# Time mixing's keys and the up projections in seven quarter products, with weight sums on GpSimd

## The chip, the cores and the metric

The kernel runs on one core of one Trainium2 chip. The metric is the device time of one execution in microseconds. The kernel's matmul, vector, activation and GpSimd engines are called TensorE (PE), VectorE (DVE), ScalarE (ACT) and GpSimd (POOL) below; SyncE (SP) issues the loads of the weights.

## The reference

All is fp32. A sequence of 256 tokens with 1024 features passes through two blocks. The first has window attention, spatial gating, pooling, memory attention and a feed-forward. The second puts 16 meta tokens in front (272 tokens) and has two layers, RWKV-7 time mixing and stick-breaking attention, each followed by a feed-forward with a short convolution. What the change touches is this:

```
# time mixing: keys
xk = x + (token_shift(x) - x) * mix[2]
k = xk @ w_k                                   # 272 x 1024 by 1024 x 1024
kk = heads(k * k_k); kk = kk / max(norm(kk), 1e-12)

# feed-forward, once per layer
u = rms_norm(h) @ w_up                         # by 1024 x 5632
u = conv_width_3(u, per channel) + conv_b
gate, val = split(u)
h = h + (silu(gate) * val) @ w_down            # 2816 x 1024
```

## The kernel before

Features lie on the 128 partitions and tokens along the free axis. All weights are one stream of blocks of 128 x 1024 (512 KB), which SyncE loads in order into a ring of eight; block b is loaded as soon as block b-8 is used. A block holds the weights of one output tile of 128 features: 8 k tiles of 128 x 128. The order of all work is written out by hand, engine by engine, with semaphores: `second_tensor`, `second_vector` and `second_scalar` hold the queues of the second block.

**Full products.** `tiles` (and the inner loop of `ffn`) does one output tile as 8 matmuls of 272 columns (260 in the last layer, where 12 meta tokens are no longer needed). The results wait in a PSUM bank for VectorE.

**Seven products.** A pair of output tiles, seen as a 2 x 2 matrix of quarters (k in two interleaved halves, output tiles in two), times x in quarters (k halves, token halves) is done as seven quarter products (Strassen-Winograd) instead of eight. `Seven` holds the layout: first block, tokens of a half, PSUM banks for even and odd pairs, first pair `i0`, and `step`. `weight_sums` makes four sums of weight quarters for each pair (lines 865, 867, 868, 870, 128 x 512 each) into one of two buffers; `x_sums` makes four sums of x once; `seven_products` issues 7 x 4 matmuls of half the columns (136 or 130) and waits for the sums before the products 6, 7 and 3; ScalarE copies the first product (`keep_first_product`, line 852), and VectorE puts the quarters together (`quads_scaled`, lines 1574 to 1580: five additions that read PSUM and one product with the norm's root). TensorE may begin pair i when pair i-2 has been taken (`taken`). Before the change the keys of time mixing are eight full tiles, and in the up projections, with F2 = 22 pairs (a gate tile and a value tile each), every odd pair is done in seven (`step` 2) and every even one in full.

**Feed-forward, up stage.** For pair m VectorE takes the result from PSUM times the norm's root (line 1643, or `quads_scaled`), for odd m makes the weight sums of pair m+2, then waits for ScalarE's first tap with bias (line 1312), adds two taps for each of the two tiles (line 1651, four instructions), waits for ScalarE's silu (line 1315) and multiplies (line 1659). After m = 3, 7, 11, 15, 19 and 21 it makes the x sums of the down projection (lines 875 to 878). In the last two pairs it makes the first two of the down projection's weight sums. The down projection (`seven_products(.., down)`) has 11 k tiles a half, in groups of 4, 4 and 3; each group waits for its x sums and its weight sums.

**Time mixing around the keys.** TensorE: r tiles 4 to 7 with the small products (`lora_out`) between, the eight key tiles, the first value tile, a sum over heads of the squared keys (16 small matmuls, `kk_sum`), more value tiles, and the chunked scan. VectorE copies r, scales and scans the decays (line 1439), takes the keys (line 1444), scales them (line 1446). ScalarE does three exponentials (line 1253 and next) after the scans and squares the keys (line 1257).

GpSimd has 32 instructions in the whole kernel, all in the first block and before time mixing.

Of the kernel before, what the change touches and what calls it, by code (L numbers as in the profile page):

```python
# [32 lines left out]
GB = 4  # L33
# [187 lines left out]
def program(nc, stream, x_t, mem_t, meta_t, cols_d, consts_d, sinks_d, ws_t, b_sp, w_pool,  # L221
            w1_d, a1_d, g1_d, w2_d, a2_d, g2_d, out_t):
    with ExitStack() as ctx:
# [142 lines left out]
        for name, y, sums in (("gate", Seven(FIRST["in"] + 18, P, [4], (0, 2), TIGHT, 0, GATES, 0, True), 1),  # L366
                              ("upq", Seven(FIRST["up"], P, [4], (3, 0), WIDE_UP, UH // 2, FF // 2, -UH, True), 1),
                              ("down", Seven(FIRST["down"], P, [4] * 4, (4, 0), SPLIT, 0, 4, 0, True), 4),
                              ("rw_o", Seven(FIRST["rw_o"], T2, [4], (0, 4), SPLIT, 1, 4, GB, True), 1),
                              ("ffa_up", Seven(FIRST["ffa_up"], T2, [4], (0, 4), WIDE, 1, F2, GB, True, 2), 1),  # L370
                              ("ffa_down", Seven(FIRST["ffa_down"], T2, [4, 4, 3], (4, 0), SPLIT, 0, 4, 0, True), 6),
                              ("sb_k", Seven(FIRST["sb_k"], T2, [4], (4, 0), WIDE, 1, 4, GB, True), 1),
                              ("sb_q", Seven(FIRST["sb_v"], L2 // 2, [4], (4, 0), WIDE, 0, 4, GB, False), 2),
                              ("sb_o", Seven(FIRST["sb_o"], L2 // 2, [4], (0, 4), SPLIT, 1, 4, GB, True), 1),
                              ("ffb_up", Seven(FIRST["ffb_up"], L2 // 2, [4], (0, 4), WIDE, 1, F2, GB, True, 2), 1),
                              ("ffb_down", Seven(FIRST["ffb_down"], L2 // 2, [4, 4, 3], (4, 0), SPLIT, 0, 4, 0, True), 6)):
            y.pair0, y.group0, y.sums0 = n_pairs, n_groups, n_sums
            SEVEN[name] = y
            n_pairs, n_groups = n_pairs + len(y.pairs()), n_groups + len(y.groups) * len(y.pairs())
            n_sums += sums  # L380

# [114 lines left out]

        def x_quarters(name):
# [31 lines left out]
        act2m = Marks(sem("time_mix_act"), "tw heads_kept tg tg1 kk_squared tg1_moved kk_root")  # L529
# [81 lines left out]
        def second_tensor(pe, mm, tiles, total):  # L611
# [73 lines left out]
            for n in range(KT):  # L685
                tiles("rw_k", FIRST["rw_k"] + n, 1, xm[1], L, j0=n)
            pe.wait_ge(ev["rw_k"], GB + 8)
            pe.wait_ge(mixed, 3)

            def value_block(n, at, freed):  # L690
                tiles("rw_v", FIRST["rw_v"] + n, 1, xm[2], L, j0=n)
                if n == 0:
                    act2m.wait(pe, "tg1_moved")
                lora_out(16 + n, beside(at), freed, g2s, tg0[:, :], g2t, tg1[0:32, :])
# [66 lines left out]
            def ffn(name, i, before):  # L761
# [3 lines left out]
                for m in range(F2):  # L765
                    if m % 2:
                        if m == 3:
                            pe.wait_ge(rooted, 10 + i)
                        seven_products(pe, mm, up, only=m)
                        continue  # L770
                    for s in (2 * m, 2 * m + 1):
                        b = FIRST[up] + s
                        arrived(pe, b)
                        if s == 1:
                            pe.wait_ge(ev[before], GB + 8)
                        elif m:
                            pe.wait_ge(ev[up], GB + s - 3)
# [34 lines left out]
        def seven_products(pe, mm, name, second=None, only=None, within=None):  # L812
# [5 lines left out]
            for i in y.pairs() if only is None else (only,):  # L818
# [4 lines left out]
                for g, n in enumerate(y.groups):  # L823
# [11 lines left out]
                    for p in ORDER:  # L835
                        if p in (6, 7, 3):
                            pe.wait_ge(w_summed, done + {6: 2, 7: 3, 3: 4}[p])
# [16 lines left out]
        def weight_sums(dve, tt, name, i, g):  # L854
# [15 lines left out]
            tt(s4, a12, s2, ALU.subtract).then_inc(w_summed, 1)  # L870

# [344 lines left out]
        def second_scalar(act, link, f, root):  # L1216
# [33 lines left out]
            for n in range(KT):  # L1250
                if n == 2:
# [4 lines left out]
                act.wait_ge(ev["rw_k"], GB + n + 1)  # L1256
                last = f(xx[:, n, :], k2[:, n, :], ACT.Square, scale=col("k_k", n))
                if n == KT - 1:
                    act2m.reach(last, "kk_squared")
            act.wait_ge(used, FIRST["rw_k"] + 8)  # L1260
            act2m.reach(cp(tg1[0:32, :], tg1_first[0:32, :]), "tg1_moved")
            value_kept(0)
# [36 lines left out]
        def ffn_scalar(act, f, root, name, layer, which):  # L1299
# [5 lines left out]

            for m in range(F2):
                if m % 2:
                    keep_first_product(act, name + "_up", m)
# [5 lines left out]
                act.wait_ge(conv_done, layer * 2 * F2 + 2 * m + 1)  # L1314
                f(cu[:, (2 * m) % 4, :], cu[:, (2 * m) % 4, :], ACT.Silu).then_inc(ffs, 1)  # L1315
# [84 lines left out]
        def second_vector(dve, link, v, tt, stt, ts, inverse_root, take):  # L1400
# [34 lines left out]
            take_r(4, KT)  # L1435
# [4 lines left out]
            link(ins)  # L1440
            tt(epre, cum, lw, ALU.subtract).then_inc(decays_summed, 1)
            for n in range(KT):
                dve.wait_ge(used, FIRST["rw_k"] + n + 1)
                cpv(k2[:, n, :], gps(n % GB)).then_inc(ev["rw_k"], 1)
                dve.wait_ge(ev["rw_k"], GB + n + 1)
                ts(kkn[:, n, :], k2[:, n, :], col("k_k", n), None, ALU.mult)
# [180 lines left out]
        def ffn_vector(dve, link, tt, stt, name, layer, quads_scaled):  # L1627
# [7 lines left out]
            for m in range(F2):  # L1635
                if m % 2:
                    quads_scaled(up, m, uu[:, (2 * m) % 4:(2 * m) % 4 + 2, :])
                    if m + 2 < F2:
                        weight_sums(dve, tt, up, m + 2, 0)
                else:  # L1640
                    for s in (2 * m, 2 * m + 1):
                        dve.wait_ge(used, b + s + 1)
                        tt(uu[:, s % 4, :], gps(3 + 4 * (s % 2), width), rs[:, 0:width], ALU.mult).then_inc(ev[up], 1)
                if m >= F2 - 2:
                    weight_sums(dve, tt, down, 0, m - F2 + 2)
                for s in (2 * m, 2 * m + 1):
                    dve.wait_ge(ffc, layer * 2 * F2 + s + 1)
                    for back, tap in ((1, 1), (2, 0)):
# [4 lines left out]
                        if back == 1:  # L1653
                            link(ins)
                        else:
                            ins.then_inc(conv_done, 1)
                dve.wait_ge(conv_done, layer * 2 * F2 + 2 * m + 2)
                dve.wait_ge(ffs, layer * F2 + m + 1)
                tt(act2[:, m, :], cu[:, (2 * m) % 4, :], cu[:, (2 * m + 1) % 4, :], ALU.mult).then_inc(ffm, 1)
                if m % 4 == 3 or m == F2 - 1:  # L1660
                    dve.wait_ge(ffm, layer * (2 + F2) + 2 + m + 1)
                    x_sums(link, tt, down, slice(m // 4 * 2, (m + 1) // 2))

# [983 lines left out]
        def _(pool):  # L2647
# [38 lines left out]
            for n in range(2):  # L2686
# [7 lines left out]
                else:  # L2694
                    pool2.reach(ins, "wa_scaled")

# [83 lines left out]
```

## Time and profile before

| | us |
|---|---|
| median of 3 runs (1451.17 to 1454.74) | 1454.0 |
| the profiled execution, own time | 1446.48 |
| its span | 1444.7 |
| TensorE busy | 1410.2 (98%) |
| TensorE weight loads (beside the products) | 1288.4 (89%) |
| VectorE busy | 911.2 (63%) |
| ScalarE busy | 326.7 (23%) |
| GpSimd busy | 26.6 (2%) |
| mean granted TensorE clock, share of full | 0.994 |
| DMA | 190.73 MB, mean 132 GB/s |

Busy times are of the span, from one profiled execution. Stages by TensorE's timeline: time mixing from 528 to 775, keys from 570.1 to 600.2, first feed-forward's up stage from 816.9 to 969.9, second one's from 1217.7 to 1365. An engine's idle time costs nothing unless another engine waits for what it does.

### The profile page before, as it was taken

To read this page: it belongs to the slowest core of one execution; us is meant where nothing else is said; L and a number is where in the kernel's file an instruction comes from. 1 tells how busy PE (TensorE), PEld (TensorE's weight loads), DVE (VectorE), ACT (ScalarE), POOL (GpSimd) and SP (SyncE) were. 2 spreads that over 40 slices of the span, in tenths; PEclk is the share of its full clock that TensorE was granted. 3 is DMA by queue.
4 is the path that set the end of the run, shared out by engine and by line. 5 is a ranking of instruction groups with operands and counts; after the bars stand their busy time and mean duration, and the time that the engine had idled before them with its cause. 6 is when DMAs were issued, how large, how long until landed. Compare 5 with 4: busy or idle time off the path is not lost.

```text
span 1444.7 us, 30444 instructions
## 1 busy us (share of the span) xinstructions
PE 1410.2 (98%) x12960; PEld 1288.4 (89%) x12960; DVE 911.2 (63%) x1836; ACT 326.7 (23%) x656; POOL 26.6 (2%) x32
## 2 busy tenths in 40 slices
PE   9999999999999999998899999999999999999997
PEld 8899888999999977778787989999997779999997
DVE  3288433358865473568544887887684447878875
ACT  2134103250000131420121222220103642222211
POOL 0140000000001000000000000000000000000000
PEclk9999999999999999999999999999998999999999
DMA  9435344355444413320000444445543114445451
GB/s 371 161 133 166 113 161 145 117 165 193 166 163 169 158 50 128 131 88 4 5 4 2 147 160 137 169 147 175 187 137 116 52 36 137 158 145 174 149 192 69
DMA packets 56992, 190.73 MB, mean 132 GB/s; under 512 B 9216, under 2 KB 11392, under 8 KB 56608
## 3 DMA queue, kind: packets, MB, share of 16 engines
q1 hardware_dynamic: 50768, 180.93, 37.1%
q10 hardware_dynamic: 6096, 7.91, 1.7%
q8 instruction: 102, 1.67, 0.5%
q14 instruction: 26, 0.21, 0.0%
HBM read 187.77 MB, written 1.05 MB: 131 GB/s over the span
## 4 chain that ended last, share of the span: by engine, by line
PE 93%; DVE 3%; ACT 1%; issue 1%; DMA 0%; ACTq 0%; DVEq 0%; PEldq 0%
PE ps L1886 93%; DVE arena L1674 1%; DMA arena<-in_x_t 0%; DVE arena L1701 0%; PE ps L1171 0%; DVE rs L2371 0%; ACT arena L2319 0%; DVE arena L1702 0%; DVE arena L1625 0%; PE ps L2089 0%; PE ps L1980 0%; DVE arena L1580 0%; DVE arena L865 0%; DVE arena L867 0%; DVE arena L1685 0%
## 5 line engine op out<-in xcount | busy, mean ns | idle before, releaser
L1886 PE MATMUL ps<-arena,ring 128*128 128x128 f32 (+6 forms) x4752 | 819.6, 324 | 3.0 <-PEq L806 0.8
L1886 PEld LDWEIGHTS ps<-arena,ring 128*128 128x128 f32 x4752 | 718.2, 191 | 75.5 <-issue 7.8
L1886 PE MATMUL ps<-arena 64*64 64x64 f32 (+10 forms) x6982 | 572.4, 257 | 13.9 <-issue 6.6
L1886 PEld LDWEIGHTS ps<-arena 128*128 128x128 f32 (+4 forms) x6982 | 514.7, 162 | 44.7 <-issue 23.9
L865 DVE TENSOR_TENSOR arena<-ring 128x512 f32<-128x512 f32 x100 | 69.0, 690 | 119.6 <-PE ps L1886 86.8
L852 ACT COPY arena<-ps 128x128 f32<-128x128 f32 (+2 forms) x72 | 19.2, 266 | 336.9 <-PE ps L1886 336.9
L1651 DVE SCALAR_TENSOR_TENSOR arena<-arena,cols 128x271 f32<-128x271 f32 (+3 forms) x176 | 82.8, 492 | 9.8 <-ACT arena L1312 6.7
L1886 PE MATMUL ps<-arena,consts 128*128 128x260 f32 (+9 forms) x368 | 75.1, 346 | 7.3 <-DVE arena L1829 3.0
L1312 ACT ACTIVATE arena<-arena,cols 128x272 f32<-128x272 f32 (+1 forms) x88 | 48.8, 601 | 122.8 <-DVE arena L1580 68.9
L1886 PEld LDWEIGHTS ps<-arena,consts 128*128 128x128 f32 (+3 forms) x368 | 54.3, 182 | 21.9 <-issue 3.5
L867 DVE TENSOR_TENSOR arena<-arena,ring 128x512 f32<-128x512 f32 x100 | 69.6, 696 | 3.5
L870 DVE TENSOR_TENSOR arena<-ring,arena 128x512 f32<-128x512 f32 x100 | 69.4, 694 | 0.0
L868 DVE TENSOR_TENSOR arena<-ring 128x512 f32<-128x512 f32 x100 | 68.6, 686 | 0.0
L2371 DVE RECIPROCAL rs<-rs 128x256 f32<-128x256 f32 (+2 forms) x10 | 17.9, 1786 | 32.7 <-ACT rs L2187 32.7
L1296 ACT ACTIVATE arena<-res 128x272 f32<-128x272 f32 (+1 forms) x32 | 13.6, 424 | 107.9 <-DVE res L1548 79.7
L1574 DVE TENSOR_TENSOR arena<-arena,ps 128x130 f32<-128x130 f32 (+1 forms) x29 | 8.5, 292 | 43.3 <-PE ps L1886 43.3
L1315 ACT ACTIVATE arena<-arena 128x272 f32<-128x272 f32 (+1 forms) x44 | 18.7, 425 | 67.9 <-DVE arena L1651 67.9
L1821 DVE TENSOR_TENSOR arena<-arena,ps 128x840 f32<-128x840 f32 x8 | 8.2, 1029 | 30.0 <-PE ps L1886 30.0
L1695 DVE TENSOR_TENSOR arena<-ps,consts 128x512 f32<-128x512 f32 x23 | 15.7, 688 | 12.3 <-PE ps L1886 12.1
L2277 ACT ACTIVATE arena<-arena 128x256 f32<-128x256 f32 (+1 forms) x12 | 5.8, 486 | 74.4 <-DVE arena L2514 66.0
L1580 DVE TENSOR_TENSOR arena<-arena,rs 128x520 f32<-128x520 f32 (+1 forms) x29 | 20.7, 712 | 3.0
L1701 DVE TENSOR_TENSOR arena<-arena,ps 128x512 f32<-128x512 f32 x18 | 12.3, 685 | 13.4 <-PE ps L1886 13.4
(279 smaller groups left out, 894.8 us busy)
## 6 DMA issues: line engine op xcount, KB each, us to landing
ring<-in_stream SPq DMA_DIRECT2D x342, 512.0 KB, 3.8
consts<-in_consts ACTq DMA_DIRECT2D x1, 1580.0 KB, 12.9
arena<-in_mem_t ACTq DMA_DIRECT2D x1, 1024.0 KB, 7.3
res<-in_x_t ACTq DMA_DIRECT2D x1, 1024.0 KB, 19.2
out_t<-arena SPq DMA_DIRECT2D x4, 256.0 KB, 2.5
arena<-in_x_t ACTq DMA_DIRECT2D x3, 256.0 KB, 5.0
arena<-in_g ACTq DMA_DIRECT2D x1, 640.0 KB, 5.6
arena<-in_w ACTq DMA_DIRECT2D x2, 256.0 KB, 4.5
```

What stands on the lines that cost most here:

```text
L852: nc.scalar.copy(QUADS[name][y.turn(i)][:, 0, 0:y.t], product_at(y, i, 1)).then_inc(p1_kept, 1)
L865: tt(s1, a21, a22, ALU.add).then_inc(w_summed, 1)
L867: tt(s2, s1, a11, ALU.subtract).then_inc(w_summed, 1)
L868: tt(s3, a11, a21, ALU.subtract).then_inc(w_summed, 1)
L870: tt(s4, a12, s2, ALU.subtract).then_inc(w_summed, 1)
L1312: f(cu[:, s % 4, :], uu[:, s % 4, :], ACT.Identity, scale=cols[:, wc + s:wc + s + 1], bias=cols[:, bc + s:bc + s + 1]).then_inc(ffc, 1)
L1315: f(cu[:, (2 * m) % 4, :], cu[:, (2 * m) % 4, :], ACT.Silu).then_inc(ffs, 1)
L1580: tt(dst, dst, over(rs[:, at], 2), ALU.mult).then_inc(ev[name], 2)
L1651: ins = stt(out=c, in0=uu[:, s % 4, 0:width - back], scalar=cols[:, at:at + 1], in1=c, op0=ALU.mult, op1=ALU.add)
L1695: tt(ysb[c % 2], blocks(2 * (c % 2) + 1), over(const(f"level{m}"), KT), ALU.mult).then_inc(y_masked[c % 2], 1)
L1886: return nc.tensor.matmul(out, lhs, rhs, start=start, stop=stop)
L2371: link(v.reciprocal(rs[:, 0:t], rs[:, 0:t]))
```

## The change

The keys become four pairs in seven products, with their own places for sums in space that is free then. In both up projections `step` becomes 1, so all pairs but the first (m = 0) are in seven products: 10 more pairs in each. The weight sums of pairs 2 to 21 move to GpSimd (`up_weight_sums`), which counts on a semaphore of its own; VectorE's counter is moved past them by hand (`count_gpsimd_sums`). VectorE's order in the up stage becomes: take pair m, gate product of m-2, taps of m-1; ScalarE's: copy of the first product of m, first taps of m, silu of m-1. In time mixing VectorE gets x sums, weight sums and `quads_keys`; ScalarE's squares go behind all keys, and its exponentials ahead of the copy of the last pair.

```diff
+    ("rw_k", Seven(FIRST["rw_k"], T2, [4], (0, 4), WIDE, 0, 4, GB, True), 1),
-    ("ffa_up", Seven(FIRST["ffa_up"], T2, [4], (0, 4), WIDE, 1, F2, GB, True, 2), 1),
+    ("ffa_up", Seven(FIRST["ffa_up"], T2, [4], (4, 0), WIDE, 1, F2, GB, True), 1),
-    ("ffb_up", Seven(FIRST["ffb_up"], L2 // 2, [4], (0, 4), WIDE, 1, F2, GB, True, 2), 1),
+    ("ffb_up", Seven(FIRST["ffb_up"], L2 // 2, [4], (4, 0), WIDE, 1, F2, GB, True), 1),
...
# TensorE, keys
-            for n in range(KT):
-                tiles("rw_k", FIRST["rw_k"] + n, 1, xm[1], L, j0=n)
-            pe.wait_ge(ev["rw_k"], GB + 8)
+            seven_products(pe, mm, "rw_k", lambda: pe.wait_ge(ev["lora"], GB + 16))
+            pe.wait_ge(ev["rw_k"], GB + 6)
...
# GpSimd
+        def up_weight_sums(pool, tt, name):
+            y = SEVEN[name]
+            for i in range(2, F2):
+                b, done = y.block(i), sums_before(name, i)
+                a11, a12, a21, a22 = w_quarters(b)
+                s1, s2, s3, s4 = [WSUM[name][y.group(i, 0) % 2][:, x] for x in range(4)]
+                arrived(pool, b)
+                arrived(pool, b + 1)
+                pool.wait_ge(used, y.block(i - 1 if i >= 3 else 0))
+                tt(s1, a21, a22, ALU.add).then_inc(ups_summed, 1)
+                pool.wait_ge(ups_summed, done + 1)
+                tt(s2, s1, a11, ALU.subtract).then_inc(ups_summed, 1)
+                tt(s3, a11, a21, ALU.subtract).then_inc(ups_summed, 1)
+                pool.wait_ge(ups_summed, done + 2)
+                tt(s4, a12, s2, ALU.subtract).then_inc(ups_summed, 1)
...
# ScalarE, up stage
             for m in range(F2):
-                if m % 2:
+                if m:
                     keep_first_product(act, name + "_up", m)
...
-                act.wait_ge(conv_done, layer * 2 * F2 + 2 * m + 1)
-                f(cu[:, (2 * m) % 4, :], cu[:, (2 * m) % 4, :], ACT.Silu).then_inc(ffs, 1)
+                if m:
+                    silu(m - 1)
+            silu(F2 - 1)
...
# VectorE, keys
+            dve.wait_ge(mixed, 3)
+            x_sums(link, tt, "rw_k")
+            take_r(4, 5)
+            weight_sums(dve, tt, "rw_k", 0, 0)
+            take_r(5, 6)
+            weight_sums(dve, tt, "rw_k", 1, 0)
+            take_r(6, KT)
...
+            weight_sums(dve, tt, "rw_k", 2, 0)
+            quads_keys(0)
+            quads_keys(1)
+            weight_sums(dve, tt, "rw_k", 3, 0)
             tt(epre, cum, lw, ALU.subtract).then_inc(decays_summed, 1)
+            quads_keys(2)
+            scaled_keys(0, 6)
...
+            quads_keys(3)
+            scaled_keys(6, 8)
# VectorE, up stage
+            for m in range(F2):
+                if m:
+                    quads_scaled(up, m, uu[:, (2 * m) % 4:(2 * m) % 4 + 2, :])
+                else:
+                    for s in range(2):
+                        dve.wait_ge(used, b + s + 1)
+                        tt(uu[:, s, :], gps(3 + 4 * s, width), rs[:, 0:width], ALU.mult).then_inc(ev[up], 1)
+                if m >= 2:
+                    gate(m - 2)
+                if m >= 1:
+                    convolve(m - 1)
+                if m >= F2 - 2:
+                    weight_sums(dve, tt, down, 0, m - F2 + 2)
+            gate(F2 - 2)
+            convolve(F2 - 1)
+            gate(F2 - 1)
```

## Rows read from the trace of the kernel before

**Rows 1.** The page: busy time by engine, and the chain that ended last.
```profile
PE 1410.2 (98%) x12960; PEld 1288.4 (89%) x12960; DVE 911.2 (63%) x1836; ACT 326.7 (23%) x656; POOL 26.6 (2%) x32
...
PE 93%; DVE 3%; ACT 1%; issue 1%; DMA 0%; ACTq 0%; DVEq 0%; PEldq 0%
```
**Rows 2.** Timeline, TensorE, first up stage: start, us, engine, line, operation, count.
```profile
831.65 8.42 PE L1886 MATMUL ps<-arena,ring 128*128 128x272 f32 x40
839.91 2.02 PE L1886 MATMUL ps<-arena 128*128 128x136 f32 x16
...
845.47 8.42 PE L1886 MATMUL ps<-arena,ring 128*128 128x272 f32 x40
```
**Rows 3.** Timeline, TensorE, second up stage.
```profile
1232.12 8.07 PE L1886 MATMUL ps<-arena,ring 128*128 128x260 f32 x40
1240.03 1.95 PE L1886 MATMUL ps<-arena 128*128 128x130 f32 x16
...
1245.39 8.07 PE L1886 MATMUL ps<-arena,ring 128*128 128x260 f32 x40
```
**Rows 4.** Timeline, VectorE, first up stage.
```profile
824.66 1.85 DVE L2371 RECIPROCAL rs<-rs 128x272 f32<-128x272 f32 x1
...
831.85 0.30 DVE L1574 TENSOR_TENSOR arena<-arena,ps 128x136 f32<-128x136 f32 x1 [1.31 <-PE ps L1886]
...
833.61 0.72 DVE L1580 TENSOR_TENSOR arena<-arena,rs 128x544 f32<-128x544 f32 x1
834.25 0.68 DVE L865 TENSOR_TENSOR arena<-ring 128x512 f32<-128x512 f32 x1
...
836.78 1.97 DVE L1651 SCALAR_TENSOR_TENSOR arena<-arena,cols 128x271 f32<-128x271 f32 x4
838.79 0.44 DVE L1659 TENSOR_TENSOR arena<-arena 128x272 f32<-128x272 f32 x1
...
936.01 0.44 DVE L875 TENSOR_TENSOR arena<-arena 128x272 f32<-128x272 f32 x1
...
937.67 0.78 DVE L1643 TENSOR_TENSOR arena<-ps,rs 128x272 f32<-128x272 f32 x2
```
**Rows 5.** Timeline, all engines but TensorE, where GpSimd works; last, groups by form.
```profile
86.15 0.73 POOL L2671 TENSOR_TENSOR arena<-arena 128x256 f32<-128x256 f32 x1
86.21 0.42 DVE L2417 TENSOR_TENSOR arena<-arena,ps 128x256 f32<-128x256 f32 x1
...
439.21 0.69 DVE L868 TENSOR_TENSOR arena<-ring 128x512 f32<-128x512 f32 x1
439.44 1.37 POOL L2690 TENSOR_TENSOR arena<-arena,small 128x512 f32<-128x512 f32 x1
439.83 1.52 DVE L870 TENSOR_TENSOR arena<-ring,arena 128x512 f32<-128x512 f32 x1
440.88 1.37 POOL L2691 TENSOR_TENSOR arena<-arena,small 128x512 f32<-128x512 f32 x1
442.33 1.04 POOL L2690 TENSOR_TENSOR arena<-arena,small 128x512 f32<-128x512 f32 x1
...
L2653 POOL TENSOR_TENSOR arena<-arena 128x512 f32<-128x512 f32 x1 | 1.3, 1267 | 0.1
```
**Rows 6.** Timeline, TensorE, VectorE and ScalarE around the keys.
```profile
570.06 29.60 PE L1886 MATMUL ps<-arena,ring 128*128 128x272 f32 x128
600.20 3.93 PE L1886 MATMUL ps<-arena,ring 128*128 128x272 f32 x16 [0.53 <-DVE arena L1444]
...
605.17 1.12 PE L1886 MATMUL ps<-arena,consts 128*32 128x272 f32 x16
...
577.37 2.42 DVE L1441 TENSOR_TENSOR arena<-arena 128x2176 f32<-128x2176 f32 x1
...
581.46 1.28 ACT L1253 ACT_TABLE_LOAD   x1
582.75 2.02 ACT L1253 ACTIVATE arena<-arena 128x2176 f32<-128x2176 f32 x1
```

More of the change, by code:

```diff
@@ L380, in program, with sums_by_gpsimd, sums_before @@
             n_sums += sums
+        ups_summed = sem("up_weights_summed")
+        def sums_by_gpsimd(name, i):
+            return name in ("ffa_up", "ffb_up") and i >= 2
+        def sums_before(name, i):
+            return 4 * ((F2 - 2) * (name == "ffb_up") + i - 2)
         def product_at(y, i, p, more=1):
@@ L1249, in second_scalar @@
                 lora_kept(j, 4 + j % GB)
-            for n in range(KT):
-                if n == 2:
+            for i in range(4):
+                if i == 3:
                     act.wait_ge(decays_summed, 1)
@@ L1255, in second_scalar @@
                     f(epre, epre, ACT.Exp).then_inc(decays_up, 1)
[L1256 to L1259, printed above, removed]
+                keep_first_product(act, "rw_k", i)
             act.wait_ge(used, FIRST["rw_k"] + 8)
             act2m.reach(cp(tg1[0:32, :], tg1_first[0:32, :]), "tg1_moved")
+            for n in range(KT):
+                act.wait_ge(ev["rw_k"], GB + 2 * (n // 2) + 2)
+                last = f(xx[:, n, :], k2[:, n, :], ACT.Square, scale=col("k_k", n))
+            act2m.reach(last, "kk_squared")
             value_kept(0)
@@ L1434, in second_vector, with quads_keys, scaled_keys @@
             mix(3, 2)
-            take_r(4, KT)
+            dve.wait_ge(mixed, 3)
[5 more added lines that the diff above has]
+            take_r(6, KT)
+            def quads_keys(i):
+                y = SEVEN["rw_k"]
+                q = QUADS["rw_k"][y.turn(i)]
+                p1, u2, uv = q[:, 0, :], q[:, 1, :], q[:, 2:4, :]
+                quarters = k2[:, 2 * i:2 * i + 2, :].rearrange("p a (b t) -> p (a b) t", b=2)
+                two = lambda p: product_at(y, i, p, 2).rearrange("p (a t) -> p a t", a=2)
+                dve.wait_ge(used, y.block(i + 1))
+                dve.wait_ge(p1_kept, y.pair(i) + 1)
+                link(tt(u2, p1, product_at(y, i, 6), ALU.add))
+                tt(quarters[:, 2, :], p1, product_at(y, i, 2), ALU.add)
+                link(tt(uv, two(7), over(u2, 2), ALU.add))
+                tt(quarters[:, 0:4:3, :], uv, two(4), ALU.add)
+                tt(quarters[:, 1, :], uv[:, 0, :], product_at(y, i, 5), ALU.add).then_inc(ev["rw_k"], 2)
+            def scaled_keys(n0, n1):
+                dve.wait_ge(ev["rw_k"], GB + n1)
+                for n in range(n0, n1):
+                    ts(kkn[:, n, :], k2[:, n, :], col("k_k", n), None, ALU.mult)
             dve.wait_ge(ev["lora"], GB + 15)
@@ L1440, in second_vector @@
             link(ins)
+            weight_sums(dve, tt, "rw_k", 2, 0)
+            quads_keys(0)
+            quads_keys(1)
+            weight_sums(dve, tt, "rw_k", 3, 0)
             tt(epre, cum, lw, ALU.subtract).then_inc(decays_summed, 1)
[L1442 to L1446, printed above, removed]
+            quads_keys(2)
+            scaled_keys(0, 6)
+            dve.wait_ge(ev["lora"], GB + 16)
             link(tt(same_head, ident, const("centre"), ALU.subtract))
             ts(same_head, same_head, 64.0, None, ALU.mult)
+            quads_keys(3)
+            scaled_keys(6, 8)
             dve.wait_ge(ev["lora"], GB + 16)
@@ L1634, in ffn_vector, with convolve @@
             up, down = name + "_up", name + "_down"
[L1635 to L1645, printed above, removed]
+            count_gpsimd_sums(dve, up)
+            def convolve(m):
                 for s in (2 * m, 2 * m + 1):
@@ L1656, in ffn_vector, with gate @@
                             ins.then_inc(conv_done, 1)
+            def gate(m):
                 dve.wait_ge(conv_done, layer * 2 * F2 + 2 * m + 2)
```

30 lines of the change are left out of this document (24 added, 6 removed).

## The prediction

> **What bounds the kernel now.** I read the page's busy line and chain of waits first. TensorE is busy for 98% of the span and carries 93% of the chain that ends last; VectorE has 3% [rows 1]. So a change pays what it takes off TensorE's own stream, as long as nothing else becomes late. The second view is the timeline of TensorE, for the price of a pair of output tiles in both forms. One fp32 matmul stands there as two instructions, so a full pair (2 tiles, 8 k, 272 columns) is 32 and a pair in seven products (7 products, 4 k, 136 columns) is 56. From 831.65 to 845.47 a full pair and a pair of seven follow one another without a gap: 13.82 us. In it the six products after the first take from 839.91 to 845.47, 5.56 us or 0.927 each, so seven take 6.49 and the full pair 7.33 [rows 2]. In the second feed-forward (260 columns) the same pattern takes 13.27, with six products in 5.36: 6.25 for seven, 7.02 for the full pair [rows 3]. The third view is VectorE's timeline of one pair, since each pair of seven gives VectorE work [rows 4].
>
> **Part 1, the keys.** Eight key tiles go from 570.06 to 599.66 (29.60 us, of which the 128 instructions need 29.3) and then TensorE waits until 600.20 for the last tile to be copied [rows 6]. Four pairs of seven at 6.49 end at 596.0; the next matmul waits only for pair 2, long taken. That is 4.2 us earlier. New VectorE work there is four quarter sums and 16 weight sums at 0.6 each; I queue them by the code: two sets lie in VectorE's idle time beside the r tiles, set 2 goes at 577.34, where the scans end (L1441 starts at 577.37 [rows 6]), and set 3 at 585.0, done 587.5, before pair 3 starts at 589.5. None is late. What moves is ScalarE: its three exponentials wait for decays_summed, now at 589.9 instead of 579.8. They took 2.0 each behind a table load of 1.28 [rows 6], 7.2 in all with their overlap, so they end at 597.1, and the copy of pair 3's first product, queued behind them, makes VectorE's last quads end at 599.2 and the squares of the keys at 601.3. TensorE wants these for the kk sum, which stood at 605.17 [rows 6], at 600.6: 0.7 lost. The kk sum then runs at 601.4, so I take **-3.8 us** (ends: -4.2 with no wait; -1 if the reciprocal on VectorE that follows the kk sum is late too). Value and scan stages keep their order behind it.
>
> **Part 2, the products of the up projections.** Ten more pairs in each. 10 x (7.33 - 6.49) = 8.4 and 10 x (7.02 - 6.25) = 7.7: **-16.1 us** [rows 2, 3]. Parts 1 and 2 together: -19.9, if all is hidden.
>
> **Part 3, VectorE beside them.** Per pair it now needs: the quarter sums and the scaling, 831.85 to 834.25, 2.40; the four taps, 836.78 to 838.79, 2.01; the gate product at 838.79, 0.4; and every fourth pair the sums for the down projection, 936.01 to 937.67, 1.66, a quarter of it 0.42 [rows 4]. That is 5.2 of the 6.49 us that a pair now lasts (5.0 of 6.25 in the second). So with the weight sums (834.25 to 836.78, 2.53 [rows 4]) gone to GpSimd, VectorE has 1.3 us a pair to spare; with them it would have had 7.7, too much.
>
> **Part 4, GpSimd and what it does to VectorE.** This decides the sign. 20 pairs in each stage, 4 additions of 512 each: 160 instructions. Undisturbed, GpSimd takes 1.04 us for such a one (two inputs, 512), and 1.27 in another place [rows 5]. Four with 0.08 between them are 4.5 to 5.4 us, under 6.49, and TensorE needs a set only a pair later: GpSimd alone is no bound.
> But the two engines are not independent. At 439.83 VectorE's L870, always 0.69 otherwise, takes 1.52 and ends at 441.35. GpSimd's addition of 512 ran from 439.44 to 440.81, itself 1.37 instead of 1.04: it began to read when L868 had read its last element, about 439.8. Of such an instruction some 0.53 us go by its elements (0.68 for 512, 0.44 for 272 [rows 4]), so L870 read from about 440.7. GpSimd's next, at 440.88, again took 1.37: it sat behind L870 [rows 5]. The two take turns, a whole instruction at a time, and GpSimd holds the way for about 0.9 us of its 1.04. At 86.15 a GpSimd addition ran beside VectorE's L2417, whose one operand is in PSUM, and neither was longer (0.73, 0.42) [rows 5]: it holds for VectorE instructions with both inputs in SBUF.
> The Trainium skill (SBUF — State Buffer, Who interferes with whom) says the same: a VectorE instruction with two SBUF inputs contends with a GpSimd instruction that reads SBUF, and whoever has the shared port pair keeps it for the whole instruction. This speaks against the change more than GpSimd's own speed does, and by that rule the trace agrees. GPSIMD Engine Reference, Engine selection, puts elementwise work on VectorE because GpSimd is about 2x slower with two inputs; here 1.04 against 0.69 is 1.5x, and by its 2x (1.38 an instruction, an estimate from that page) a set would take 5.8, still under a pair.
> Which of VectorE's 5.2 us can be stopped? The five quarter sums read PSUM (1.76 us, 831.85 to 833.61 [rows 4]); the scaling by rs, the taps, the gate and the down sums read only SBUF: 3.4 us, two thirds. A GpSimd instruction that meets them costs VectorE at most its 0.9, and about 0.75 since start and tail of VectorE's instructions lie beside it. Bounds per pair: 0, and 4 x 0.9 = 3.6. I take two thirds of 4 x 0.75: 2.0. VectorE then needs **7.2 us a pair** against TensorE's 6.49, and 7.0 against 6.25 in the second. TensorE may not start pair i before pair i-2 is scaled (two sets of banks), so VectorE may be 6.49 - 2.45 = 4 us late and then sets the pace; and what it is late at the end, the down projection waits for, since its sums stand in the same queue. So the lag is paid in full: 20 x 0.7 = 14 and 20 x 0.75 = 15, **+29 us**.
>
> **Part 5, start and end of each up stage.** GpSimd's first set starts with the stage (its weights are there), just where VectorE does weight sums and x sums, ready at 824.66 for a pair of seven that starts at 831.65 - 6.49 = 825.16 [rows 2, 4]: 0.5 to spare. Four turns at about 0.5 cost 2.1: +1.6 each. At the end the order gate(m-2), taps(m-1) leaves two tap groups and two gates, and both weight sets of the down projection (2 x 2.53), behind the last pair. By the queue the second set's second sum comes at 9.0 us after the last pair, and TensorE wants it at 6.49 + 0.93 = 7.4: +1.6 each. Bounds 0 and 4 each. Together **+6.4 us**. The new order on ScalarE (activation one pair later) I cost at nothing: it is busy for 23% of the span [rows 1].
>
> **Sum.** -3.8 - 16.1 + 29 + 6.4 = **+16 us** on the profiled execution (span 1444.7, its own time 1446.5), thus 1462 there. Taken on the median shown, 1454.0, which is 7.5 above that execution: **about 1471 us**, 1.1% slower.
>
> **Rivals.**
> A, the forecast: VectorE, stopped by GpSimd, paces both up stages. For: the turns that the two engines took, three of them in one place [rows 5]. Against: the 2.0 us of blocking is worked out, not seen, and the sign turns at about 1.35 us a pair. Its own range is 1460 to 1488. Chance 0.58.
> B, other side: the stops fall mostly beside the PSUM reads and in the 1.3 us to spare, since each GpSimd set starts when a pair ends, as the quarter sums do. If VectorE's lag stays under 4 us, only start and end cost: -19.9 + 3 to 6, about **1438 to 1441**. It decides if blocking is under 1.3 us a pair (1.25 in the second). For: the first two of four additions do start beside the quarter sums. Against: the other two then meet scaling, gate and taps, and every fourth pair has no room at all (4.8 + 1.66 = 6.4). Chance 0.27.
> C, in between: one stage paced by VectorE and not the other, or blocking near 1.4: 1448 to 1459. Chance 0.07.
> D, GpSimd at 1.27 an addition as in its slowest case: 1.1 held, 2.6 blocked a pair, 0.6 x 40 = 24 more: about **1495**. GpSimd itself would use 5.4 plus its own stops, close to the 6.49. Chance 0.08.
>
> **Numbers.** Predicted is A: 1471. The range runs from B to A's end: 1437 to 1490; it leaves out D and little else. A measurement here tells 0.3% (4.4 us) from no change. Faster is B, 0.27. Same is half of C and little more, 0.07. Slower 0.66.
>
> **What would show it.** For A: waits of TensorE in both up stages for the scaling at L1580, in pieces of 1 to 4 us and mostly behind the pairs with down sums; the taps' mean up from 0.49 to 0.7 or more, GpSimd's additions at 1.1 to 1.3. For B: no such waits, taps under 0.65. Part 1 is right if the first value tile starts some 26 us after the first key product and ScalarE's last copy of a first key product comes right after the exponentials. Part 5 is right if TensorE waits once at the first pair of seven and once in the second group of the down projection. The prediction is wrong at its root if VectorE's SBUF-only instructions in the up stages keep their durations.

## The result, and the profile after

The changed kernel took **1509.9 us** (median of 4 runs, 1507.5 to 1512.1) against 1452.6 for the kernel before (4 runs, 1445.3 to 1454.7): a ratio of 1.041, 95% interval 1.038 to 1.044. It is slower by 57 us; 1471 was predicted, with 1490 as the upper end. The direction was right, the size was not, and the time lies outside the range.

The page of the changed kernel: the busy line, and the chain that ended last by engine and by line.

```profile
PE 1418.1 (94%) x13536; PEld 1318.9 (87%) x13536; DVE 1020.5 (68%) x1868; ACT 326.8 (22%) x680; POOL 249.9 (17%) x192
...
PE 73%; DVE 20%; issue 5%; ACT 1%; DMA 0%; DVEq 0%; ACTq 0%; SPq 0%; PEldq 0%
```

TensorE's share of the chain fell from 93% to 73% and VectorE's rose from 3% to 20% [rows 1]. VectorE's busy time rose by 109 us. Its own work fell by 80 weight sums in the up stages and rose by 16 for the keys and 24 sets of quarter sums; the added and the spared work nearly cancel, and the rise is instructions that last longer.

Where the time went is read from TensorE's timeline: the first product of the sums over features at the start of each stage marks it. Of the changed kernel, start and duration:

```profile
816.47 1.08 PE L1972 MATMUL ps<-arena,consts 128*128 128x272 f32 x4
...
1070.35 1.08 PE L1972 MATMUL ps<-arena,consts 128*128 128x272 f32 x4
```

That is the first feed-forward, 253.9 us; the marks of the second stand at 1249.80 and 1499.02, 249.2 apart. The same marks of the kernel before stand 224.3 and 213.6 apart. So the two feed-forwards lost 29.6 and 35.7 us, 65 together, and all else together gained 1.

What TensorE waited for most (the changed kernel; us in total, times, longest), and some of the waits themselves in the first feed-forward (x8 is eight instructions, which are four matmuls):

```profile
PE ps L1972 <- DVE arena L1656: 47.9, 12, 6.2
```

```profile
823.56 1.17 PE L1972 MATMUL ps<-arena,ring 128*128 128x136 f32 x8 [2.35 <-DVE arena L919]
...
877.91 2.18 PE L1972 MATMUL ps<-arena,ring 128*128 128x136 f32 x8 [5.02 <-DVE arena L1656]
...
977.86 2.18 PE L1972 MATMUL ps<-arena,ring 128*128 128x136 f32 x8 [5.04 <-DVE arena L1656]
...
1002.42 2.12 PE L1972 MATMUL ps<-arena 128*128 128x136 f32 x16 [1.21 <-DVE arena L888]
```

L1656 is the scaling by the root (L1580 before), L919 the last x sum, L888 the second of the four weight sums of a set of the down projection. The list has no wait of TensorE for a GpSimd sum: GpSimd's sums are never late. After two smaller ones at 858.51 and 866.14 the waits come every fourth pair (877.91, 910.66, 944.08, 977.86), 5 us each, and between 877.91 and 977.86 twelve pairs pass: 8.33 us a pair, where TensorE needs 6.49 and the forecast had 7.2. In the second feed-forward the same waits stand at 1309.52 and 1411.58: 8.51 a pair, where 7.0 was forecast.

VectorE in 850 to 990, grouped by form (count | busy us, mean ns):

```profile
L1719 DVE SCALAR_TENSOR_TENSOR arena<-arena,cols 128x271 f32<-128x271 f32 x34 | 29.1, 856 | 0.0
L1719 DVE SCALAR_TENSOR_TENSOR arena<-arena,cols 128x270 f32<-128x270 f32 x34 | 25.9, 761 | 1.2
L1656 DVE TENSOR_TENSOR arena<-arena,rs 128x544 f32<-128x544 f32 x17 | 19.0, 1116 | 1.8
L1729 DVE TENSOR_TENSOR arena<-arena 128x272 f32<-128x272 f32 x17 | 17.0, 999 | 0.0
L1653 DVE TENSOR_TENSOR arena<-arena,ps 128x272 f32<-128x272 f32 x17 | 7.5, 439 | 0.6
...
L917 DVE TENSOR_TENSOR arena<-arena 128x272 f32<-128x272 f32 x4 | 5.6, 1395 | 0.1
```

The quarter sums, which read PSUM, kept their duration (L1653: 439 ns, the same as a 272-column instruction had before). All that takes both its inputs from SBUF is longer: the taps 0.81 instead of 0.50, the scaling 1.12 instead of 0.72, the gate product 1.00 instead of 0.44 [rows 4]. Per pair that is 1.24 for four taps, 0.39 for the scaling and 0.56 for the gate; the four down sums of every fourth pair (L916 to L919) took 4.7 instead of 1.66, 0.71 a pair (12 us over 17 pairs). Together **2.9 us a pair**, against the 2.0 of the forecast. The second feed-forward gives 3.1 by the same sum (1281 to 1415, 16 pairs).

The other engine, GpSimd's weight sums over the whole kernel (lines 906, 908, 909 and 911, 40 sets; L909 has 1475 and L906 1369 ns), and a piece of both engines' timelines, GpSimd first:

```profile
L911 POOL TENSOR_TENSOR arena<-ring,arena 128x512 f32<-128x512 f32 x40 | 59.0, 1475 | 0.0
...
L908 POOL TENSOR_TENSOR arena<-arena,ring 128x512 f32<-128x512 f32 x40 | 53.6, 1340 | 3.1
```

```profile
886.34 1.27 POOL L906 TENSOR_TENSOR arena<-ring 128x512 f32<-128x512 f32 x1 [7.37 <-PE ps L1972]
887.69 1.27 POOL L908 TENSOR_TENSOR arena<-arena,ring 128x512 f32<-128x512 f32 x1
888.92 1.75 POOL L909 TENSOR_TENSOR arena<-ring 128x512 f32<-128x512 f32 x1
```

```profile
882.84 0.73 DVE L1656 TENSOR_TENSOR arena<-arena,rs 128x544 f32<-128x544 f32 x1
883.48 0.43 DVE L1729 TENSOR_TENSOR arena<-arena 128x272 f32<-128x272 f32 x1
883.84 1.98 DVE L1719 SCALAR_TENSOR_TENSOR arena<-arena,cols 128x271 f32<-128x271 f32 x4
...
887.97 1.58 DVE L1656 TENSOR_TENSOR arena<-arena,rs 128x544 f32<-128x544 f32 x1
889.47 1.50 DVE L1729 TENSOR_TENSOR arena<-arena 128x272 f32<-128x272 f32 x1
```

Until 886.34 GpSimd is idle and VectorE's instructions last as before. From then on it works; its first addition meets the quarter sums, which read PSUM, and the same two instructions behind them last 1.58 and 1.50. Undisturbed, an addition takes GpSimd **1.27 us, not 1.04**. Both figures stood in [rows 5].

### The profile page after: what moved, and what is told of

Same layout as the page of the kernel before. It is cut to its first block, busy times and chain, and to the rows that moved or that the text cites. A ratio compares the mean times of both kernels' runs of the same rounds, so it can differ in the third digit from the quotient of the medians.

```text
span 1508.8 us, 31889 instructions
## 1 busy us (share of the span) xinstructions
PE 1418.1 (94%) x13536; PEld 1318.9 (87%) x13536; DVE 1020.5 (68%) x1868; ACT 326.8 (22%) x680; POOL 249.9 (17%) x192
## 4 chain that ended last, share of the span: by engine, by line
PE 73%; DVE 20%; issue 5%; ACT 1%; DMA 0%; DVEq 0%; ACTq 0%; SPq 0%; PEldq 0%
PE ps L1972 72%; DVE arena L1719 5%; DVE arena L1729 2%; DVE arena L1656 1%; DVE arena L1653 1%; DVE arena L918 1%; DVE arena L917 1%; DVE arena L919 1%; DVE arena L1652 1%; DVE arena L916 1%; DVE arena L1651 1%; DVE arena L1650 1%; DVE arena L1760 1%; DVE arena L886 1%; DVE arena L888 1%
## 5 line engine op out<-in xcount | busy, mean ns | idle before, releaser
L1972 PE MATMUL ps<-arena,ring 128*128 128x128 f32 (+6 forms) x4560 | 735.7, 311 | 55.8 <-DVE arena L1656 47.9
L1972 PEld LDWEIGHTS ps<-arena,ring 128*128 128x128 f32 x4560 | 652.1, 194 | 104.9 <-DVE arena L1656 50.8
L1972 PE MATMUL ps<-arena 64*64 64x64 f32 (+8 forms) x7750 | 684.8, 262 | 17.4 <-issue 7.5
L1972 PEld LDWEIGHTS ps<-arena 128*128 128x128 f32 (+4 forms) x7750 | 620.8, 168 | 48.9 <-issue 25.0
L906 POOL TENSOR_TENSOR arena<-ring 128x512 f32<-128x512 f32 x40 | 54.7, 1369 | 738.2 <-PE ps L1972 738.2
L1719 DVE SCALAR_TENSOR_TENSOR arena<-arena,cols 128x271 f32<-128x271 f32 (+3 forms) x176 | 135.5, 790 | 3.1
L888 DVE TENSOR_TENSOR arena<-arena,ring 128x512 f32<-128x512 f32 x84 | 59.5, 708 | 2.9
L911 POOL TENSOR_TENSOR arena<-ring,arena 128x512 f32<-128x512 f32 x40 | 59.0, 1475 | 0.0
L909 POOL TENSOR_TENSOR arena<-ring 128x512 f32<-128x512 f32 x40 | 59.0, 1475 | 0.0
L1656 DVE TENSOR_TENSOR arena<-arena,rs 128x520 f32<-128x520 f32 (+1 forms) x49 | 51.4, 1050 | 5.5 <-DVE arena L1654 0.5
L908 POOL TENSOR_TENSOR arena<-arena,ring 128x512 f32<-128x512 f32 x40 | 53.6, 1340 | 3.1
L1729 DVE TENSOR_TENSOR arena<-arena 128x272 f32<-128x272 f32 (+1 forms) x44 | 38.0, 864 | 0.1
```

The source lines that it names most:

```text
L888: tt(s2, s1, a11, ALU.subtract).then_inc(w_summed, 1)
L906: tt(s1, a21, a22, ALU.add).then_inc(ups_summed, 1)
L908: tt(s2, s1, a11, ALU.subtract).then_inc(ups_summed, 1)
L909: tt(s3, a11, a21, ALU.subtract).then_inc(ups_summed, 1)
L911: tt(s4, a12, s2, ALU.subtract).then_inc(ups_summed, 1)
L1656: tt(dst, dst, over(rs[:, at], 2), ALU.mult).then_inc(ev[name], 2)
```

## The experiments

Each run is compared with the kernel before on the same chip. "Expected" is what was put on record before the run, "stages" the changes of the first and the second feed-forward against before, by the marks above, from each run's profile. Executions of one kernel spread by up to 16 us (e6, 12 runs: 1437.9 to 1454.3).

| run | expected us | median us | ratio to before (95%) | stages |
|---|---|---|---|---|
| the changed kernel | about 1471 | 1509.9 | 1.041 (1.038 to 1.044) | +29.6, +35.7 |
| e1 keys only | 1448.5 | 1444.3 | 0.996 (0.994 to 0.998) | 0, 0 |
| e2 sums over 32 of 512 | 1433 to 1441 | 1429.4 | 0.986 (0.981 to 0.992) | -6.8, -5.6 |
| e3 writes, no reads | 1433 to 1442 | 1435.9 | 0.989 (0.984 to 0.993) | -6.8, -5.6 |
| e5 root in PSUM | 1496 to 1506 | 1489.5 | 1.026 (1.022 to 1.031) | +24.4, +18.1 |
| e8 one operand twice | 1470 to 1485 | 1478.7 | 1.018 (1.012 to 1.024) | +13.8, +16.0 |
| e4 all sums on VectorE | 1484 to 1492 | 1479.4 | 1.019 (1.016 to 1.022) | +13.3, +16.5 |
| e6 17 pairs in seven | 1441 to 1446 | 1440.8 | 0.996 (0.993 to 0.998) | -2.0, +1.1 |
| e7 15 pairs in seven | 1442 to 1445 | 1446.3 | 0.996 (0.994 to 0.998) | -1.0, -0.2 |
| e9 as e6, weight set early | 1435 to 1437, or 1441 | 1444.3 | 0.996 (0.994 to 0.998) | -1.9, 0.0 |
| e10 as e7, weight set early | about 1442, or 1446 | 1449.2 | 0.999 (0.996 to 1.001) | -0.9, +1.5 |

e2, e4 and e5 came out 4 to 7 us below what was expected (e4 and e5 in every execution), and no run shows why; e7 came out 1 us above.

### e1: the keys alone

The feed-forwards are those of the kernel before; only the keys are in seven.

> The kernel before with the keys of time mixing in four pairs of seven products, nothing else of the change. The first value tile started 30.14 us after the first key product before and 26.05 after, so 4.1 us should be won and kept: 1448.5, ratio 0.997. If the value and scan stages behind it take the gain back: ratio 1.000.

Measured: 1444.3 against 1451.2 (12 and 29 runs), -6 us by the ratio (-3 to -9). The term of the forecast, -3.8, lies inside. The mark behind the scan stage varies by 10 us between profiles of kernels that agree up to there (813.3 in e1, 823.6 in e3), so the changed kernel's own timeline is the finer measure:

```profile
571.89 1.20 PE L1972 MATMUL ps<-arena,ring 128*128 128x136 f32 x8
...
597.94 3.83 PE L1972 MATMUL ps<-arena,ring 128*128 128x272 f32 x16
601.61 1.27 PE L1972 MATMUL ps<-arena 128*128 128x272 f32 x4
602.81 1.12 PE L1972 MATMUL ps<-arena,consts 128*32 128x272 f32 x16
```

The first value tile starts 26.05 us after the first key product, against 30.14 [rows 6], and the kk sum follows 30.92 after it against 35.11, with no wait: -4.2.

### e2 and e3: the sums made small, or without reads

```
+                few = [x[:, :, 0:8] for x in (s1, s2, s3, s4, a11, a12, a21, a22)]
+                s1, s2, s3, s4, a11, a12, a21, a22 = few
```

> The changed kernel, but GpSimd's four sums of each pair cover 8 of 128 columns of a quarter (32 elements instead of 512); the rest of the sum buffers holds old values. Same instructions, waits and order on all engines, hardly any reading by GpSimd. Theory T (GpSimd's reads stop VectorE's instructions with both inputs in SBUF, a whole instruction at a time, and VectorE so slowed paces both up stages): almost all of the loss goes, 1433 to 1441 us, taps at L1719 back to 0.50 mean, no waits of TensorE for the scaling at L1656. Rival R (the new order on VectorE and ScalarE, or seven products in all pairs, is too much for VectorE by itself): stays above 1480. Rival G (GpSimd is late with its sums): also about 1437, so it needs the next run.

```
-                tt(s1, a21, a22, ALU.add).then_inc(ups_summed, 1)
+                nc.gpsimd.memset(s1, 0.5).then_inc(ups_summed, 1)
```

(and so for s2, s3, s4)

> The changed kernel with GpSimd's four sums replaced by four fills of the same 512 elements (it writes the buffers and reads nothing); values of the sums are not made. T: writing does not stop VectorE's reads, 1433 to 1442 us although GpSimd still has 160 instructions of full width. If any work of GpSimd slows VectorE, also writing: above 1470, taps above 0.65 us.

In e2 the waits for the scaling are gone and the order of all queues is the changed kernel's. The only waits of the up stages left in it:

```profile
PE ps L1974 <- DVE arena L888: 2.6, 2, 1.4
```

They stand at the ends of the two stages; at their starts none is left. So neither the new order nor the amount of VectorE's own work made the changed kernel slow: with GpSimd's reads away it is 1.4% faster than before, and 80 us faster than with them. In e3 GpSimd works on the same 128 x 512, but only writes. GpSimd's and VectorE's groups (of the whole kernel):

```profile
L911 POOL MEMSET arena<- 128x512 f32 x40 | 21.1, 527 | 0.0
...
L1719 DVE SCALAR_TENSOR_TENSOR arena<-arena,cols 128x271 f32<-128x271 f32 x44 | 21.8, 495 | 0.0
```

The taps last what they lasted before, and so does the scaling (725 ns) [rows 4]. It is the reads that stop VectorE, not these writes (a fill is also shorter, 0.53 us against the addition's 1.27, but 2.1 us of fills a pair lengthen nothing). The Trainium skill (SBUF — State Buffer, Who interferes with whom) says this of a VectorE instruction with two SBUF inputs: it contends with a GpSimd instruction that reads SBUF and not with one that only writes it. By that rule the trace agrees.

### e5: the scaling reads its root from PSUM

```
-                    quads_scaled(up, m, uu[:, (2 * m) % 4:(2 * m) % 4 + 2, :])
+                    quads_scaled(up, m, uu[:, (2 * m) % 4:(2 * m) % 4 + 2, :], gps(3, width))
+                    dve.wait_ge(ev[up], GB + 2)
+                    link(nc.vector.tensor_copy(gps(3, width), rs[:, 0:width]))
```

> The changed kernel; VectorE copies the norm's root once into a PSUM bank that is free after the first pair and takes it from there when it scales each pair, so this instruction (L1656, 544 elements, 1.12 mean in the middle of the first up stage against 0.72 undisturbed) has one SBUF input instead of two. T: it goes back to 0.73 while GpSimd works beside it; part of the stop moves to the gate product and the taps behind it: 0.2 to 0.4 us a pair are won, 1496 to 1506 us. If it is not the inputs in SBUF that matter but VectorE's time in general: L1656 stays above 1.0 and the time within 0.3% of the changed kernel's 1509.

```profile
L1719 DVE SCALAR_TENSOR_TENSOR arena<-arena,cols 128x271 f32<-128x271 f32 x44 | 40.0, 909 | 0.0
...
L1656 DVE TENSOR_TENSOR arena<-arena,ps 128x544 f32<-128x544 f32 x21 | 15.1, 721 | 2.2
```

The scaling, in the two up stages 1.10 on average with both inputs in SBUF, takes 0.72 (0.70 in the second) again, as when nothing disturbs it; the taps behind it are still stopped, and more. The gain is 20 us, more than the 4 to 14 expected. Over both up stages the scaling is 17 us shorter than in the changed kernel, the gate products are 10 and the down sums 4 shorter, and the taps 15 longer: 16 us less on VectorE. The waits for the scaling became 15, the longest 4.2 instead of 6.2; shorter waits also leave TensorE fewer slow matmuls (below), which would explain the rest, but no run separates it.

### e8: GpSimd's additions with one operand read twice

```
-                tt(s1, a21, a22, ALU.add).then_inc(ups_summed, 1)
+                tt(s1, a21, a21, ALU.add).then_inc(ups_summed, 1)
```

(and so for the others)

> The changed kernel; each of GpSimd's four sums takes one of its operands twice (a21+a21 and so on), so the values of the sums differ, the number of elements does not. In the changed kernel an undisturbed sum takes 1.26, while the rows of the forecast had 1.04 for 512 elements where both operands were nearly the same addresses or one was a few broadcast values. If that is what makes 1.04 of 1.26: mean undisturbed duration 1.04, blocking about 2.0 to 2.4 a pair instead of 2.9, and the time falls to 1470 to 1485, near the forecast. If two reads are two reads wherever they go: 1.26 again and 1509 within 0.5%.

Its timeline, GpSimd (first undisturbed, then not) and VectorE beside it:

```profile
853.98 1.04 POOL L908 TENSOR_TENSOR arena<-arena 128x512 f32<-128x512 f32 x1
854.98 1.52 POOL L909 TENSOR_TENSOR arena<-ring 128x512 f32<-128x512 f32 x1
```

```profile
854.66 0.94 DVE L1656 TENSOR_TENSOR arena<-arena,rs 128x544 f32<-128x544 f32 x1
855.53 1.27 DVE L1729 TENSOR_TENSOR arena<-arena 128x272 f32<-128x272 f32 x1
```

This is the forecast's assumption made true: an undisturbed addition of 1.04 us (in three of the four lines; the fourth, L911, was never under 1.22). The gate product behind one lasts 1.27 instead of 0.43, 0.84 more, where the forecast allowed 0.75. By the same sum as above VectorE is stopped for 2.2 us a pair in the first stage (850 to 990) and 2.3 in the second (1275 to 1400). The time, 1478.7, is 7.7 above the 1471 predicted and inside the forecast's own range (1460 to 1488). 31 of the 39 us that the forecast missed hang on what one addition costs, with what follows from longer stops.

### e4: all sums on VectorE

GpSimd has no sums; VectorE makes the set of pair m+2 after it has taken pair m, as in the kernel before, for all pairs but the first.

```
+            def sums_of_nth(n):
+                if n < len(SEVEN[up].pairs()):
+                    weight_sums(dve, tt, up, SEVEN[up].pairs()[n], 0)
...
                     quads_scaled(up, m, uu[:, (2 * m) % 4:(2 * m) % 4 + 2, :])
+                    sums_of_nth(SEVEN[up].nth(m) + 2)
```

> The changed kernel with all weight sums of the up projections on VectorE, two pairs ahead, right after it has taken a pair; GpSimd does none. VectorE then needs 5.2 + 2.5 = 7.7 us a pair for certain, against 5.2 plus a measured 2.9 of stops with GpSimd. T: GpSimd costs VectorE more than it takes off it, so this is faster than the changed kernel: 20 x 1.25 and 20 x 1.3 us of lag on 1432.4 (all hidden), and 3 at the ends: 1484 to 1492. Rival (GpSimd relieves VectorE, the loss lies elsewhere): slower than 1510.

It is faster than the changed kernel by 30 us, although VectorE does all the work, and 5 us faster than was expected. TensorE's waits for the scaling in its first up stage:

```profile
873.44 1.19 PE L1998 MATMUL ps<-arena,ring 128*128 128x136 f32 x8 [0.95 <-DVE arena L1674]
...
965.09 1.19 PE L1998 MATMUL ps<-arena,ring 128*128 128x136 f32 x8 [1.80 <-DVE arena L1674]
```

Two more stand between them, the longest 2.02. Twelve pairs in 91.65 us are 7.64 a pair; the forecast said 7.7 for this case and dismissed it. In the changed kernel GpSimd takes 2.5 us a pair of work from VectorE and gives back 2.9 of stops.

### e6, e7, e9 and e10: fewer pairs in seven

With all sums on VectorE, full pairs are put back where it would be late: `FULL = (0, 5, 9, 13, 17)` in e6, `FULL = (0, 3, 6, 9, 12, 15, 18)` in e7.

> Keys in seven; in each up projection 17 of 22 pairs in seven (full ones: 0, 5, 9, 13, 17) instead of 11, all weight sums on VectorE, GpSimd none, order of the changed kernel. TensorE: 4.1 + 6 x 0.84 + 6 x 0.77 = 13.8 less. VectorE: 17 x 7.7 + 5 x 3.6 = 149 us against TensorE's 147 in a stage: about 2 us late at each end, plus 1 to 2 for the sums of the down projection. T: 1441 to 1446, ratio 0.992 to 0.996. If VectorE at its limit loses more than the sum says (chains between engines): 1450 or more.

> As the one with seventeen, with 15 of 22 pairs in seven (full: 0, 3, 6, 9, 12, 15, 18). TensorE: 4.1 + 4 x 1.61 = 10.5 less. VectorE: 15 x 7.7 + 7 x 3.6 = 141 of 149 us, so it is not late in the stage: 1442 to 1445, ratio 0.993 to 0.995; the three pairs of seven at the end, with both weight sets of the down projection, may cost 1 to 2.

Both have the ratio of e1: the six and four additional pairs of a stage brought next to nothing. Their waits in the middle of the stage are gone, what is left stands at its end. Of e6 (e7 has the same at 970.86, 1.90 us, and in the second stage 2.20):

```profile
968.67 2.12 PE L1998 MATMUL ps<-arena 128*128 128x136 f32 x16 [2.20 <-DVE arena L906]
```

L906 belongs to the down projection's second weight set, behind a gate product, four x sums and four taps in VectorE's queue (4.0 us, 963.18 to 967.20, not the 5.3 of the expectation below). In e9 and e10 it goes ahead of them:

```
+                if m == F2 - 1:
+                    weight_sums(dve, tt, down, 0, 1)
                 if m >= 2:
                     gate(m - 2)
```

> Keys and 17 of 22 pairs in seven as in the run with full pairs 0, 5, 9, 13, 17, all sums by VectorE; only the down projection's second weight set moves ahead of the gate product, the sums of activations and the taps that stood before it in the last pair (5.3 us of VectorE's queue). If the order at the end of the up stage is what took the rest of the gain, TensorE's waits for L906 (5.7 us, 3 times, longest 2.3 in that run) fall under 2 us and the time is 4 to 6 us less than that run's 1440.8: about 1435 to 1437. If VectorE's load itself is the limit there, the wait comes back a pair later, for the sums of activations, and the time stays within 2 us of 1441.

> The same move in the kernel with full pairs 0, 3, 6, 9, 12, 15, 18 (15 of 22 in seven). If the order at the end is the cause, its waits for L906 (4.1 us, 2 times) go and the stages, -1.0 and -0.2 us against before, come to about -3.2 and -2.3: the time some 4 us under that run's 1446.3 or, by the profiles' spans, 1436. By the rival it stays.

```profile
979.72 0.93 PE L2000 MATMUL ps<-arena,ring 128*128 128x136 f32 x6 [2.00 <-DVE arena L937]
980.96 1.66 PE L2000 MATMUL ps<-arena 128*128 128x136 f32 x12 [0.30 <-DVE arena L906]
```

The wait of e9 stands one group later, for the last x sum (L937), and is nearly as long, and its first stage gains as much as that of e6: the rival's mechanism is there, at 1444.3 instead of the 1441 that it gave. e10 has the same waits (1.70 and 2.10 us). What VectorE has left after the last pair is more than TensorE's next work covers, in both orders that were tried. The kernel before, whose VectorE has less to do there, has no such wait in either feed-forward. In e6 the stages fall 3.0 and 5.7 us short of what TensorE's sums gave, 8.7 together. The three waits for L906 are 5.7 of it. Another 1.6 are slow matmuls behind the last of them: at 1363.04 sixteen instructions took 3.51 instead of 1.95. The remaining 1.4 stays unexplained. By the ratios none of the four is told apart from e1, so **the keys alone are the version to keep**: 0.4% faster than before, with nothing added to the up projections.

## Why the prediction was right or wrong

**Part 1, the keys: right.** -3.8 was said, -4.2 measured, since the kk sum did not wait. The expected order on ScalarE is there: the exponentials run from 592.31 to 598.14 and the copy of the last first product stands right behind them, at 598.05.

**Part 2, TensorE's own saving: right.** The pairs go at 6.49 and 6.25 wherever nothing stops them. e2 shows it nearly whole: -12.4 in the two stages against the saving of -16.1. Of the missing 3.7 the waits for L888 at the two ends are 2.6; nothing waits at the starts, and 1.1 stays open.

**Part 3, VectorE's own need: right.** 5.2 a pair; in e2 taps, scaling and gate last what was taken, and no wait for the scaling is left.

**Part 4, the stops: the mechanism right, the size wrong, and this is the step that failed.** Turns of whole instructions, only against VectorE instructions that take both inputs from SBUF, waits of TensorE for the scaling behind the pairs with down sums (5 us, where 1 to 4 were said), taps at 0.7 or more: all there (taps 0.79). The failed term is what one addition costs, "Undisturbed, GpSimd takes 1.04 us for such a one", and with it the 0.75 of a stop and the 2.0 of a pair: the additions take 1.27 undisturbed, and 1.34 to 1.48 on average in the four lines. So one stop costs 1.0 us or more (the gate 1.07, a down sum 0.96), not 0.75, and VectorE loses 2.9 a pair, not 2.0. I had both figures in [rows 5], for the same shape of 128 x 512, and took the lower. What tells them apart is what they read: the 1.27 adds two separate operands, as the weight sums do; the 1.04 has a few broadcast values or nearly the same addresses as its second operand. e8 shows it on the weight sums themselves: the same operand twice 1.04, two operands 1.27. The Trainium skill (GPSIMD Engine Reference, Elementwise — side-by-side cycle accounting) puts GpSimd at about 2.6 cycles an element against VectorE's one, and its measured ratio for a two-input addition is 1.96. The ratio here is 1.27 to 0.69, 1.8, nearer to that page's than the 1.5 that I had set against it.

Rival D had this mechanism (1.27 an addition, 2.6 blocked) with a chance of 0.08 and a price of 1495. It should have been the forecast. Its price was also too low: 2.9 and 3.1 are blocked a pair, not 2.6, 16 us over 40 pairs. That 1495 and these 16 come so near the measured time is partly luck, since two further errors (below) partly cancel.

Two figures of the prediction do not follow from its own sums. With 1.29 and 1.25 us to spare a pair and 6.4 for start and end, the sign turns at 1.6 us of stops a pair, not at 1.35, so the forecast's 2.0 stood nearer to the turn than it says. And 1454.0 + 16 is 1470, not 1471.

**What no part had: TensorE after a long wait.** By VectorE's stops alone a pair of the first stage would last 5.2 + 2.9 = 8.1; it lasts 8.33. Behind each wait of about 5 us TensorE's next matmuls were slow, in the changed kernel's timeline:

```profile
910.66 2.18 PE L1972 MATMUL ps<-arena,ring 128*128 128x136 f32 x8 [5.03 <-DVE arena L1656]
912.63 3.26 PE L1972 MATMUL ps<-arena 128*128 128x136 f32 x16
915.73 1.09 PE L1972 MATMUL ps<-arena,ring 128*128 128x136 f32 x8
```

Eight instructions in 2.18 instead of 1.09 and sixteen in 3.26 instead of 2.02. The granted clock was 0.50 of full from 910.70 to 912.60, the lower of its two levels, and 0.59 on average from 912.70 to 915.70: it was low from the first instruction behind the wait on, and then rose again. Four such pieces in the first stage and five in the second take 21 us more than the same instructions undisturbed. So TensorE's own account of the two feed-forwards is 47.9 us of waits for the scaling, 6.5 of waits at start and end and 21 of slow instructions, less the 16.1 saved: 59 of the 65 us lost, and 6 stay open. VectorE in turn waits for the pair that runs slowly. Columns of the next rows: stretch, its length, busy time of PE, PEld, DVE, ACT, POOL, granted clock, DMA share, GB/s; the changed kernel.

```profile
850.00:990.00 140.00, 116.95 (x921) 115.74 (x920) 130.97 (x203) 28.47 (x68) 90.23 (x64) 0.91 0.35 124
1251.00:1436.00 185.00, 157.19 (x1260) 154.54 (x1259) 166.60 (x269) 37.55 (x88) 104.82 (x76) 0.92 0.36 129
```

The granted clock was 0.91 and 0.92 of full, and 1.00 in the same stage of the kernel before; in e4 it was 0.99 in both stages, and behind the four waits of its first stage's pairs, 2.0 us at most, the eight instructions took 1.19. VectorE waited for TensorE: 4.5 us over 17 pairs in the first stage, 5.2 over 12 in the second, 0.27 and 0.44 a pair. All of these waits stand behind a slow piece; the four of the first stage are 0.40, 1.07, 1.42 and 1.59 us, each 1.1 less than what its slow piece had lost (1.50, 2.18, 2.53, 2.70). So the paces add up: 5.2 + 2.9 + 0.27 = 8.4 (measured 8.33), and 5.0 + 3.1 + 0.44 = 8.5 (8.51). Against the forecast's 7.2 and 7.0 this is 20 x 1.1 and 20 x 1.5, 53 us; the two feed-forwards exceed the forecast by 46 (65.3 against 19.3). The difference would be lag that is never paid, since TensorE can run on until VectorE is 4 us late and the forecast gave nothing for that; this is argued, no run shows it. Of the excess, e8 shows 31 us to hang on the addition's length; how much of it comes by way of the slow matmuls is worked out (0.27 and 0.44 by 20, some 14 us), and no run separates it.

**Part 5, start and end: right in sum.** 6.4 was said; the waits at start and end are 2.35 and 1.21 in the first stage, 1.54 and 1.40 in the second, 6.5 together. Those at the starts are gone in e2 and e3, so GpSimd's reads made them, as was said; those at the ends stay there (1.19 and 1.39 in e2) and come from the new order, where 1.6 each was said.

**Rival B** (hidden, 1438 to 1441) is what the kernel does when the reads are away, and a little faster: e3 1435.9, e2 1429.4. Its price had 3 to 6 us for start and end, and without the reads nothing waits at the starts.

## What to carry to other kernels

Before work is moved from VectorE to GpSimd, price what it stops there: for every GpSimd instruction that reads SBUF, one VectorE instruction of the same moment that takes both inputs from SBUF can be late by most of the GpSimd instruction's length (here up to 1.07 of 1.27 us). Where VectorE is near the bound with such instructions (here 3.4 of 5.2 us a pair), the move can cost it more than it relieves (here 2.9 against 2.5 us a set). Where a trace has two durations for one shape, find out what differs before taking one, and take the row whose operands are like those of the new instruction. And when a new producer comes close to the pace of the engine that it feeds, add what comes behind each long wait: TensorE's clock can have fallen, and here its slow instructions cost 1.5 to 2.9 us at a time.

## What was not expected of the hardware

- A GpSimd addition of 128 x 512 takes 1.27 us with two separate operands and 1.04 with the same operand twice (e8), and a memset of the same size 0.53 (e3).
- TensorE's first eight instructions behind the changed kernel's eight waits of 4.7 to 6.2 us took 2.1 to 2.2 us instead of 1.1, at a granted clock of 0.50. Behind shorter waits both occur: 1.20 behind 2.08 us in its first stage and 1.91 behind 2.05 in its second, 2.18 and 1.19 behind 2.97 in e8, 1.86 and 1.16 behind 4.09 in e5.
- Moving one operand of a VectorE instruction into PSUM takes it out of GpSimd's way: 0.71 instead of 1.10 us on average in the up stages (e5).
